# One gate and query matmul of 512 columns in the neighbourhood attention of a fused two-block kernel

## The reference

```python
# o_w_in: 2048 x (4 * 2048), for q, k, v and the gate; 32 heads of 64
q, k, v, z = projections of rmsnorm(h)
s   = q_row . k_rows * scale + bias        # masked to 16 columns around the query
s_m = q_row . k_meta * scale               # meta tokens are seen by every query
o   = softmax([s, s_m]) @ [v_rows, v_meta]
h   = h + (o * silu(z)) @ o_w_out          # then the final norm; the meta rows are cut off
```

## Time and profile before

| what | value |
|---|---|
| median of 3 runs | 2341.41 us (2339.06 to 2342.9) |
| the profiled execution's own time | 2339.95 us |
| its span | 2338.2 us |
| PE busy | 2312.7 us, 99% of the span |
| DVE busy | 1800.9 us, 77% |
| ACT busy | 1198.8 us, 51% |
| POOL busy | 582.1 us, 25% |
| bytes moved by DMA | 438.19 MB, mean 187 GB/s |

### The profile page before, as it was taken

The page is one execution under the profiler, slowest core; times in us unless marked ns, Lnnn a source line. Parts: engine busy times, 40 slices in busy tenths (PEclk is TensorE's granted clock), DMA queues, the critical chain, the costliest instruction groups (busy, mean ns, idle before and its releaser), DMA issues.

```text
span 2338.2 us, 51146 instructions
## 1 busy us (share of the span) xinstructions
PE 2312.7 (99%) x17400; PEld 2192.0 (94%) x17400; DVE 1800.9 (77%) x3189; ACT 1198.8 (51%) x1735; POOL 582.1 (25%) x421
## 2 busy tenths in 40 slices
PE   8999999999999999999999999999999999999997
PEld 8999888998898889899999999999999999999997
DVE  6777888888888766689888889999873566666666
ACT  5444455555555444447666744333544444444443
POOL 0230000000000000013423368888788311111100
PEclk9999999999999999999999999999999999999999
DMA  8644566666666666656555555555555555555444
GB/s 283 205 168 147 191 204 206 209 199 211 200 212 199 211 196 196 195 185 195 182 183 172 182 172 180 179 182 197 174 180 182 186 174 166 169 166 181 161 163 152
DMA packets 152476, 438.19 MB, mean 187 GB/s; under 512 B 32339, under 2 KB 47228, under 8 KB 152268
## 3 DMA queue, kind: packets, MB, share of 16 engines
q1 hardware_dynamic: 148844, 424.42, 55.0%
q0 software_dynamic: 3264, 12.41, 2.0%
q10 hardware_dynamic: 288, 0.30, 0.0%
HBM read 434.88 MB, written 11.09 MB: 191 GB/s over the span
## 4 chain that ended last, share of the span: by engine, by line
PE 87%; DVE 7%; issue 3%; ACT 2%; DVEq 1%; DMA 0%; SPq 0%; ACTq 0%
PE bank L1189 24%; PE bank L1172 15%; PE bank L1173 15%; PE bank L1174 15%; PE bank L1190 12%; DVE bank L2301 1%; DVE wlo L1647 1%; DVE c L2076 1%; PE bank L1430 1%; ACT whi L676 1%; PE bank L1550 1%; PE bank L1540 1%; PE bank L1530 1%; PE bank L1401 1%; PE bank L1557 0%
## 5 line engine op out<-in xcount | busy, mean ns | idle before, releaser
L676 ACT CAST whi<-raw 128x1024 fp32r<-128x1024 f32 x784 | 817.1, 1048 | 533.6 <-PE bank L1174 376.6
L1647 DVE TENSOR_TENSOR wlo<-raw,whi 128x1024 fp32r<-128x1024 f32 x624 | 762.1, 1227 | 235.0 <-ACT whi L676 221.6
L1172 PE MATMUL bank<-xhl,whi 128*128 128x272 f32 (+1 forms) x3086 | 878.0, 285 | 2.7 <-DVE xhl L1715 1.3
L1173 PE MATMUL bank<-xhl,whi 128*128 128x272 f32 (+1 forms) x3086 | 867.0, 281 | 0.0
L1174 PE MATMUL bank<-xhl,wlo 128*128 128x272 f32 (+1 forms) x3086 | 866.8, 281 | 0.0
L1172 PEld LDWEIGHTS bank<-xhl,whi 128*128 128x128 f32 x3086 | 580.5, 188 | 7.6 <-issue 2.6
L1173 PEld LDWEIGHTS bank<-xhl,whi 128*128 128x128 f32 x3086 | 580.7, 188 | 0.6 <-issue 0.2
L1174 PEld LDWEIGHTS bank<-xhl,wlo 128*128 128x128 f32 x3086 | 580.4, 188 | 0.0
L1189 PE MATMUL bank<-xhl,whi 128*128 128x512 f32 x1408 | 470.0, 382 | 0.3 <-DVE ug L1979 0.3
L614 POOL TENSOR_TENSOR wlo<-raw,whi 128x1024 fp32r<-128x1024 f32 x160 | 381.8, 2395 | 95.0 <-ACT whi L676 94.8
L1190 PE MATMUL bank<-xhl,wlo 128*128 128x256 f32 x1408 | 384.4, 273 | 0.0
(11 more groups left out here) (290 smaller groups left out, 2688.8 us busy)
## 6 DMA issues: line engine op xcount, KB each, us to landing
raw<-w_up SPq DMA_DIRECT2D x176, 512.0 KB, 4.3
raw<-w_na SPq DMA_DIRECT2D x128, 512.0 KB, 3.6
raw<-w_ssm SPq DMA_DIRECT2D x96, 512.0 KB, 3.8
raw<-w_glu SPq DMA_DIRECT2D x96, 512.0 KB, 3.5
raw<-w_down SPq DMA_DIRECT2D x80, 512.0 KB, 3.7
raw<-w_qkv SPq DMA_DIRECT2D x48, 512.0 KB, 4.3
raw<-w_mix SPq DMA_DIRECT2D x32, 512.0 KB, 3.8
raw<-w_outa SPq DMA_DIRECT2D x32, 512.0 KB, 3.5
```

Source lines behind the costliest of these rows:

```text
L676: A.copy(whi[s][:, :], raw[s][:, :]).then_inc(sem("hi_done"), 1)
L1172: T.matmul(to_, wh, xh_, start=head, stop=False)
L1173: T.matmul(to_, wh, xl_, start=False, stop=False)
L1647: V.tensor_tensor(wlo[s][:, :], raw[s][:, :], whi[s][:, :].bitcast(F32), SUB).then_inc(sem("lo_done"), 1)
```

## The change

Gate and query tiles are computed in the joined form, and the activations of `na` get a new layout. A k-tile now takes 36 lines of 16 columns (XN = 576): the high part of the 16 meta columns, the high part of the 256 tokens, the low part of the tokens (from line 17), the low part of the meta columns (line 33), and two unused lines.

- Gate and query (k = 1, 2): one matmul of 512 columns over high and low tokens, and one of 256 with the low weight.
- Value and key (k = 0, 3): still three matmuls of 272 columns. The low one writes to columns 16 to 287 of the bank, so that the low sums of the meta columns land in 272 to 287. For the first k-tile it is cut in two, 256 and 16 columns.
- DVE: `halves` copies the low sums of gate or query to `no` and adds the high ones, ahead of the multiplication, which now reads `no`. `keyed` copies the low sums of the 16 meta columns to `no` and adds the high ones. These are linked steps: 18 per pair in place of 10.
- `outb`: the low part is written by two instructions, of 256 and 16 columns.

```diff
+            def stream_na(i, j):
...
+                    if k in (1, 2):
+                        T.matmul(by_lines(pb_[:, :]), wh, by_lines(xhl[:, o + META:o + META + 2 * SEQ]),
+                                 start=kt == 0, stop=False)
+                        ins = T.matmul(by_lines(pb_[:, 0:SEQ]), wl, by_lines(xhl[:, o + META:o + TOK]),
+                                       start=False, stop=kt == 15)
+                    else:
+                        high_, low_ = by_lines(xhl[:, o:o + TOK]), by_lines(xhl[:, o + LOW:o + LOW + TOK])
+                        T.matmul(by_lines(pb_[:, 0:TOK]), wh, high_, start=kt == 0, stop=False)
+                        if kt:
+                            T.matmul(by_lines(pb_[:, META:META + TOK]), wh, low_, start=False, stop=False)
+                        else:
+                            T.matmul(by_lines(pb_[:, META:TOK]), wh, by_lines(xhl[:, o + LOW:o + LOW + SEQ]),
+                                     start=False, stop=False)
+                            T.matmul(pb_[:, TOK:TOK + META], wh, xhl[:, o + LOWMETA:o + LOWMETA + META],
+                                     start=False, stop=False)
+                        ins = T.matmul(by_lines(pb_[:, 0:TOK]), wl, high_, start=False, stop=kt == 15)
...
-                    off, n = ((0, TOK), (META, SEQ), (META, SEQ), (0, TOK))[k]
-                    stream_x("na", i, j, off, n)
+                    stream_na(i, j)
...
+                    elif phase == "outb":
+                        high_, c = tok(xhl, k, i, 2, 0, TOK, XN), vcol(gain, k, i, 2)
+                        ch.link(V.tensor_scalar(high_, tok(x, k, i, 2, 0, TOK), c, None, MUL))
+                        for at_, from_token, n_ in ((LOW, META, SEQ), (LOWMETA, 0, META)):
+                            ins = V.scalar_tensor_tensor(
...
-                V.tensor_tensor(view(to[:, 0:META], meta), view(from_[:, 0:META], twice), view(r_[:, 0:META], twice), MUL)
+                ch.link(V.tensor_copy(no[:, 0:META], from_[:, TOK:TOK + META]))
+                ch.link(V.tensor_tensor(no[:, 0:META], from_[:, 0:META], no[:, 0:META], ADD))
+                V.tensor_tensor(view(to[:, 0:META], meta), view(no[:, 0:META], twice), view(r_[:, 0:META], twice), MUL)
...
+            def halves(i, j, k):
+
+                wait_chunk_done(dve, "na", i, j)
+                from_ = pbank("na", k)
+                ch.link(V.tensor_copy(no[:, :], from_[:, SEQ:2 * SEQ]))
+                ch.link(V.tensor_tensor(no[:, :], from_[:, 0:SEQ], no[:, :], ADD))
...
-                scaled("na", i, 3, 1, nz[:, :], r1, SEQ, META)
+                halves(i, 3, 1)
+                freed("na", i, 1, V.tensor_tensor(nz[:, :], no[:, :], r1[:, META:TOK], MUL))
...
-                wait_chunk_done(dve, "na", i, 5)
-                freed("na", i, 2, V.tensor_tensor(by_blocks(qt[:, :]), by_rows(pbank("na", 2)[:, 0:SEQ]),
+                halves(i, 5, 2)
+                freed("na", i, 2, V.tensor_tensor(by_blocks(qt[:, :]), by_rows(no[:, :]),
```

More of the change, by code:

```diff
@@ L138, in program @@
         xh, xl = xhl[:, LINE:KT * XW], xhl[:, KT * XW + LINE:2 * KT * XW]
+        XN, LOW, LOWMETA = 36 * LINE, 17 * LINE, 33 * LINE
         LINES = 2 * LINE
@@ L1204, in stream_up @@
                 joined("up", i, j, j // 2, t2, ktiles(j), j % 2 == 0, j % 2 == 1)
+            def stream_na(i, j):
+                k = j // 2
+                if j % 2 == 0:
+                    pe.wait_ge(sem("bank_free"), tile("na", i, k) + 1)
+                wait_lo(pe, "na", i, j)
+                s, pb_ = j % RING, pbank("na", k)
+                for kt in ktiles(j):
+                    r, o = kt % 8, kt * XN
+                    wh, wl = whi[s][:, r * P:r * P + P], wlo[s][:, r * P:r * P + P]
+                    if k in (1, 2):
[14 more added lines that the diff above has]
+                        ins = T.matmul(by_lines(pb_[:, 0:TOK]), wl, high_, start=False, stop=kt == 15)
+                ins.then_inc(sem("chunk_done"), 1)
             def norm(n, cols=TOK):
@@ L1906, in landed @@
                              vcol(gain, k, i, 2)).then_inc(sem("xs_ready"), 1)
+                    elif phase == "outb":
[3 more added lines that the diff above has]
+                            ins = V.scalar_tensor_tensor(
+                                out=tok(xhl, k, i, 2, at_, n_, XN), in0=tok(x, k, i, 2, from_token, n_), scalar=c,
+                                in1=tok(xhl, k, i, 2, from_token, n_, XN).bitcast(F32), op0=MUL, op1=SUB)
+                        ins.then_inc(sem("xs_ready"), 1)
                     elif gain:
@@ L2483, in _ @@
             with dve.Fori(2, NPAIR) as i:
-                ch.begin(i, 10, 2)
+                ch.begin(i, 18, 2)
                 na(i, True)
```

## The result

The changed kernel took 2344.52 us, the median of 20 runs (2342.49 to 2346.63), against 2340.91 (2338.91 to 2342.9) for 20 runs of the kernel before beside them. The ratio is 1.0015, with a 95% interval of 1.001 to 1.0021: 3.6 us slower, where 3 us faster was forecast. It lies inside the 0.2% that the text called no change, but on the other side, and 0.02 us above the upper end of the range, 2344.5. The profiled execution took 2343.55 us.

What follows compares the result with a forecast made beforehand. PE (TensorE) was taken to bound the neighbourhood attention, busy 414.7 us of 415.2. The terms 5.6 + 0.5 - 2.7 - 0.4 gave 3.0 us faster, forecast 2338 against the median 2341.41, range 2333.5 to 2344.5.

Steps and rivals of the forecast that it cites:

- Gate and query k-tiles at 333.3 ns: Joined gate and query k-tiles in `na` go from 344.6 to 333.3 ns, 496 of them: 5.6 us won.
- The spacing of 36 lines changes addresses alone; `down` and `up` read lines in that pattern.: The new layout of the activations was costed at no time lost or won.
- a sign of being wrong: The prediction called itself wrong if k-tiles of value or key take over 360 ns.
- The 16-column matmul at 91 ns: First k-tile of value and key tiles: 32 added matmuls, 2.9 us less 0.2, 2.7 us lost, ends 0.2 and 3.5.
- `outb`'s third instruction: Last low write in `outb`: a step of at most 0.2 us leaves 0.4 before PE needs it, costing nothing.
- Steady pairs of DVE at nothing: DVE's added steps in steady pairs of `na`, 2.6 us of a pair's 25.8, hide behind PE and cost nothing.
- The key tile behind the query tile, 0.5 us: Starts behind the query tile lose their extra 0.03 us per pair: 0.5 us won in all.
- First pair, `nvt`, 0.4 us: In the first pair PE waits on `nvt`, with two added 16-column DVE steps on the path: 0.4 us lost.
- Joined starts gain little or nothing: Rival for gate and query: each joined start saves a small fixed cost or nothing, 2341 to 2344.5; chance 0.14.
- The other side: Rival: PE pays for switching between high and low sums 16 columns apart, 2346; chance 0.08 with other PE waits.

Runs made afterwards that it cites:

- experiment 1: Changed kernel with its new layout, but gate and query again as three 256-column matmuls per k-tile, without `halves`: 2350.34 us, ratio 1.004.
- experiments 2 and 3: experiment 2, and the changed kernel without 16-column matmuls (first high matmul 288 columns wide, low one 272 at once): the latter 2340.76 us, ratio 1.0002.
- the last two runs of 7: Kernel before, instructions kept, activations laid out in 40 lines a k-tile: at line 0 of four 2352.07 us, at line 1 of four 2343.31 us.
- experiment 8: Changed kernel with its block of activations one, two or three lines (64 bytes each) higher: 2351.93, 2347.58 and 2348.51 us.
- experiment 9: Changed kernel without 16-column matmuls, in other layouts: two runs in 34 or 40 lines, 2346.24 and 2346.02 us; high and low lines in turn, 2362.67 and 2361.69.
- experiment 5: Changed kernel without `halves`, so DVE leaves the low sums of gate and query out of the result: 2346.92 us, ratio 1.0016.
- experiment 2: Changed kernel, but `outb` writes the low part by one 272-column instruction, not by one of 256 and one of 16: 2343.57 us, ratio 1.0009.

## Why the prediction was wrong, step by step

- **Gate and query k-tiles at 333.3 ns: this step failed, with 2.7 us of the 5.9 between forecast and result.** 340.0 were measured, and the term of -5.6 came out as -2.9. The 333.3 of the earlier trace rows were read in another stage and carried over as if the pace belonged to the form alone. That joining saves something is shown (experiment 1: 4.5 us in these tiles with the layout kept). The form can reach 333: it does in the first two pairs, and in chunks 3 and 4 of experiments 2 and 3. What keeps it at 340 in the steady pairs is open.
- **"The spacing of 36 lines changes addresses alone; `down` and `up` read lines in that pattern."** This step failed as well: value and key tiles were costed at an unchanged 360 ns. The value tile lost 2.1 us: its k-tiles take 367 to 369 ns, over the 360 that the prediction had named as a sign of being wrong. The diff moved the high run from line 1 to line 0 of four and the low run to line 17. That such a move can cost this much is shown: under the old instructions one line costs `na` 7.6 us (the last two runs of 7), and under the new ones 6.1 (experiment 8, one line up). That it is what cost the value tile its 2.1 us is argued. The matmuls in between count as well (experiment 9), and the old instructions were not run in this very layout.
- **The 16-column matmul at 91 ns.** The mechanism was right, the size was off: 0.10 to 0.11 us each, 3.2 us net and not 2.7. It lay near the top of the range given, 3.5.
- **`outb`'s third instruction: "Nothing".** The 0.2 us were right for a DVE alone. POOL was splitting weights at that moment, and the instructions of `outb` took up to 2.7 us; PE lost 0.97 us, of which about 0.5 stood in for the longer wait on `nvt`. The prediction named POOL nowhere in this step.
- **Steady pairs of DVE at nothing.** Right: no wait on `nz`, `qt` or `kt`, and without the four steps of `halves` no chunk of the steady pairs differs by more than 1 ns (experiment 5).
- **The key tile behind the query tile, 0.5 us.** Right in place and size: its first chunk went from 365 to 360 ns a k-tile.
- **First pair, `nvt`, 0.4 us.** The wait is 0.4 us after, 0.5 before, because PE had already been held 0.97 us earlier. With that hold gone (experiment 2) it is 0.9: the 0.4 forecast.
- **The rivals.** "Joined starts gain little or nothing" had about the right range (2341 to 2344.5), but not the right reason: the joined k-tiles gained 2.9 us of 5.6, more than half, and the rest of the loss came from elsewhere. The other side's mechanism, PE paying for going to and fro between the high and low sums, is spoken against by the changed kernel's own key tile: its low sums lie 16 columns off, and its k-tiles behind the first take 360.0 ns. The old instructions sum high and low in the same columns, and at line 0 they are slower by 7.6 us in `na`, so it is not needed for the loss.

What stays open: why the same instructions at the same addresses run at different paces. `outb` does, between four traces and the rest. In the changed kernel k-tiles of gate and query take 333 ns in chunk 3 of the second pair and 340 in the later ones. Experiment 2, with the same matmuls and addresses in `na`, has 333 in chunks 3 and 4 and 340 in chunk 5, and its value and key tiles pay 0.14 us more a pair. The distances repeat from pair to pair within a run in a fixed pattern. So what came before a tile seems to count beside its place; this was not settled. The paces come from one trace of each kernel; the times of the other runs bear out the large differences (7.7 us), not those of 1 or 2 us. Nor was it shown which memory the effect of the address comes from; the runs moved only the activations, not weights or banks.

## What to carry to other kernels

This PE-bound stream at full pace was sensitive to the 64-byte place of its moving data. So before a layout is changed, write down at which line of four each run starts, and time the new layout under the old instructions, and shifted by one line, before anything else is judged. A pace read in another stage is a guess for this one: here it was off by 2%, which was half of the gain. Look also at the stages that the change leaves alone, since their pace can differ between two traces, and that is then no effect of the change. Price each extra matmul, however narrow, at a whole weight load (0.11 us here), and look at what POOL does under any DVE instruction that is added on a path to PE.

## What the runs showed of the hardware that I had not expected

- 64 bytes of address took 272-column matmuls from 120.0 to 124.8 ns, 7.6 us in a stage `na` of 410.
- The same matmuls of `outb`, at the same addresses, started 120.0 ns apart in 14 traces and 122.2 in four.
- Value and key matmuls of the same form and addresses took 360 or 367 ns a k-tile, with other gate and query tiles between them.
- High and low lines in turn took 381 to 419 ns a k-tile of value and key, against 360.
- A matmul of 128 or 16 columns under 128 weight columns cost 0.10 to 0.11 us either way.
- DVE's write of the low part took 0.50 us in one piece; in two pieces, of 0.23 us at the shortest, one of them took up to 2.68 us beside POOL's splits.
